# A float32 encoder trunk on one core: x read over two queues, one more block of it evicted by two engines, and the last down projection's right half summed onto the residual in PSUM

## What is computed

```python
def _rmsnorm(x, g):
    xf = x.astype(jnp.float32)
    y = xf * lax.rsqrt(jnp.mean(xf * xf, axis=-1, keepdims=True) + EPS)
    return (y * g.astype(jnp.float32)).astype(x.dtype)

for layer in range(DEPTH):
    h = _rmsnorm(x, mix_norm[layer])
    x = x + mixer(h)                 # attention in layer 0, recurrence in layer 1
    x = x + _swiglu(_rmsnorm(x, ffn_norm[layer]), ffn_w_gate_up[layer], ffn_w_down[layer])
return _rmsnorm(x, final_norm)
```

## Time and profile before

| what | value |
|---|---|
| median of three runs | 1302.98 us (1302.68 to 1303.4) |
| the profiled execution's own time | 1301.03 us |
| its span in the trace | 1299.2 us |
| PE busy | 1282.9 us, 99% |
| PEld (weight load) busy | 1028.2 us, 79% |
| POOL busy | 611.0 us, 47% |
| DVE busy | 560.6 us, 43% |
| ACT busy | 551.7 us, 42% |
| DRAM traffic | 97 GB/s over the span |

### The profile page before, as it was taken

How to read it: one execution, slowest core, us unless ns; L and a number is a source line. 1 busy time by engine, 2 the same in 40 slices (tenths; PEclk the granted TensorE clock), 3 DMA queues, 4 the chain that set the end, 5 groups by cost and what they waited for, 6 DMA issues and landing times.

```text
span 1299.2 us, 18386 instructions
## 1 busy us (share of the span) xinstructions
PE 1282.9 (99%) x6525; PEld 1028.2 (79%) x6525; DVE 560.6 (43%) x872; ACT 551.7 (42%) x1006; POOL 611.0 (47%) x487
## 2 busy tenths in 40 slices
PE   8999999999999999999999999999999999999998
PEld 6877777777778888888888876777888888888886
DVE  4866574756645512121202027999843131311011
ACT  5454444444445433333323247785533333333223
POOL 4565664646535454545444443430244444444442
PEclk9999999999999999999999999999999999999999
DMA  6522222122323333333332343214333333343322
GB/s 208 160 73 62 68 60 63 56 68 62 121 69 110 97 97 95 96 95 96 102 96 84 106 166 117 81 57 146 98 97 89 105 89 103 91 120 98 96 95 94
DMA packets 123415, 126.31 MB, mean 97 GB/s; under 512 B 7896, under 2 KB 106456, under 8 KB 122712
## 3 DMA queue, kind: packets, MB, share of 16 engines
q1 hardware_dynamic: 123320, 125.46, 32.0%
q10 hardware_dynamic: 32, 0.01, 0.0%
HBM read 119.15 MB, written 6.29 MB: 97 GB/s over the span
## 4 chain that ended last, share of the span: by engine, by line
PE 58%; issue 21%; POOL 12%; DVE 5%; ACT 3%; DMA 1%; POOLq 0%; SPq 0%; DVEq 0%; ACTq 0%
PE ps L1493 17%; PE ps L1495 16%; PE ps L1494 16%; POOL w_lo L495 11%; PE ps L1853 2%; PE ps L1611 1%; PE ps L1646 1%; PE ps L1623 1%; PE ps L1627 1%; PE ps L1588 1%; POOL rot L504 1%; PE ps L1657 1%; DMA x_tok<-in_x_dram 1%; PE ps L1665 1%; DVE bkn L1137 1%
## 5 line engine op out<-in xcount | busy, mean ns | idle before, releaser
L495 POOL TENSOR_TENSOR w_lo<-w_stage,w_hi 128x512 fp32r<-128x512 f32 (+2 forms) x430 | 543.0, 1267 | 672.6 <-ACT w_hi L555 672.4
L555 ACT ACTIVATE w_hi<-w_stage 128x512 fp32r<-128x512 f32 (+2 forms) x448 | 263.8, 594 | 574.4 <-PE ps L1495 565.2
L1493 PE MATMUL ps<-h_hi,w_hi 128*128 128x512 f32 x1104 | 439.8, 398 | 1.6 <-DVE h_lo L948 1.0
L1495 PE MATMUL ps<-h_hi,w_lo 128*128 128x512 f32 x1104 | 430.2, 390 | 0.0
L1494 PE MATMUL ps<-h_lo,w_hi 128*128 128x512 f32 x1104 | 430.1, 390 | 0.0
L1493 PEld LDWEIGHTS ps<-h_hi,w_hi 128*128 128x128 f32 x1104 | 207.3, 188 | 63.4 <-issue 16.7
L1495 PEld LDWEIGHTS ps<-h_hi,w_lo 128*128 128x128 f32 x1104 | 207.2, 188 | 43.6
L1494 PEld LDWEIGHTS ps<-h_lo,w_hi 128*128 128x128 f32 x1104 | 207.4, 188 | 43.2 <-issue 2.6
L1276 DVE TENSOR_TENSOR silu_g<-ps,rstd_wide 128x512 f32<-128x512 f32 x44 | 30.2, 686 | 327.5 <-PE ps L1495 327.5
L1493 PE MATMUL ps<-w_hi,f_hi 128*128 128x512 f32 x176 | 68.6, 390 | 0.1
L1495 PE MATMUL ps<-w_hi,f_lo 128*128 128x512 f32 x176 | 68.5, 389 | 0.0
(11 more groups left out here) (229 smaller groups left out, 1633.6 us busy)
## 6 DMA issues: line engine op xcount, KB each, us to landing
w_stage<-in_ffn_w_gate_up_dram SPq DMA_DIRECT2D x176, 256.0 KB, 3.1
w_stage<-in_ffn_w_down_dram SPq DMA_DIRECT2D x88, 256.0 KB, 2.7
w_stage<-in_even_w_in_dram SPq DMA_DIRECT2D x96, 192.0 KB, 2.5
w_stage<-in_odd_w_in_dram SPq DMA_DIRECT2D x32, 256.0 KB, 2.8
x_spill<-x_t SPq DMA_DIRECT2D x2, 2048.0 KB, 8.5
x_t<-x_spill SPq DMA_DIRECT2D x2, 2048.0 KB, 7.9
w_stage<-in_odd_w_out_dram SPq DMA_DIRECT2D x16, 256.0 KB, 2.7
w_stage<-in_even_w_out_dram SPq DMA_DIRECT2D x16, 192.0 KB, 2.4
```

The costliest lines, as they stand in the source:

```text
L495: pool.tensor_tensor(out=w_lo[:, s, 0:n], in0=stage[:, s, 0:n], in1=w_hi[:, s, 0:n].bitcast(f32), op=ALU.subtract).then_inc(chunk_lo, 1)
L555: act.activation(w_hi[:, j % RING, 0:n], stage[:, j % RING, 0:n], ACT.Copy).then_inc(chunk_hi, 1)
L1493: pe.matmul(out_, lh, rh, start=start, stop=False, skip_group_check=skip)
L1495: return pe.matmul(out_, ll, rh, start=False, stop=stop, skip_group_check=skip)
```

## The change

There are four parts.

1. SP issues x blocks 0 and 2, ACT's queue blocks 1 and 3, ahead of `mix_rows`. The turn of `mix_rows` on PE stands behind x_turn(1).
2. Block 2 of x_t is copied in halves like block 3, the left by DVE and the right by ACT.
3. ACT converts chunk 4 behind the first square of x and chunk 5 behind the second.
4. Only the left four tiles of the residual are turned back in the first group of the last FFN, into banks 2 and 3 by turns. The right four tiles are turned during the half g = 0 of the last down projection, at k = 8 to 11, straight into banks 4 to 7 (`x_under_sums`), and the products of g = 1 are accumulated onto them. So `y_sum(1, c)` goes, and the square and the scaling of the right half read PSUM.

```diff
@@ -388,7 +388,7 @@
 
             sync.dma_start(ident[:, :], A["consts"][:, K_IDENT:K_IDENT + P]).then_inc(consts_in, 16)
-            for c in range(NC):
+            for c in (0, 2):
                 sync.dma_start(x_tok[:, c, :], x_rows[c]).then_inc(x_in[c], 16)
             for c in range(C_PAIR):
@@ -420,7 +420,7 @@
                     if (p, j) == (0, 3):
                         sync.wait_ge(x_by_dve, 3)
-                        sync.wait_ge(x_by_act, 2)
+                        sync.wait_ge(x_by_act, 3)
                         sync.dma_start(x_spill, x_t[:, :, :].rearrange("p k t -> p (k t)")).then_inc(spilled, 16)
 
@@ -584,10 +584,13 @@
 
                 g, c = divmod(i, NC)
-                act.wait_ge(y_new, i + 1)
+                if g:
+                    act.wait_ge(y_summed, c + 1)
+                else:
+                    act.wait_ge(y_new, c + 1)
                 if i >= 2:
                     act.wait_ge(y_squared, i - 1)
-                act.activation(y_sq[:, i % 2, :], y_tok[c][:, g * 512:(g + 1) * 512], ACT.Square,
+                act.activation(y_sq[:, i % 2, :], ps[:, 4 + c, :] if g else y_tok[c][:, 0:512], ACT.Square,
                                accum_out=y_stat[:, g, c:c + 1]).then_inc(y_squared, 1)
 
@@ -626,6 +629,8 @@
                 act.activation(rstd_wide[:, :], ps[:, NORM_BANK[n], :], ACT.Sqrt, scale=1.0 / D, bias=eps[:, 0:1]).then_inc(norm_sqrt, 1)
 
+            for c in (1, 3):
+                act.dma_start(x_tok[:, c, :], x_rows[c]).then_inc(x_in[c], 16)
             act.dma_start(mix_rows[0:G_FFN, :], A["mix_norm"].rearrange("l (n p) -> (l n) p", p=P)).then_inc(mix_in, 16)
 
@@ -636,7 +641,7 @@
                     act.wait_ge(mix_gain_in, 1)
                     act.wait_ge(x_by_dve, 3)
-                act.wait_ge(x_by_act, 1 + k // 4)
+                act.wait_ge(x_by_act, 1 + 2 * (k // 4))
                 act.activation(h_hi[:, k, :], x_t[:, k, :], ACT.Copy, scale=params[:, G_MIX + k:G_MIX + k + 1]).then_inc(h_hi_done, 1)
 
@@ -648,6 +653,8 @@
             act.wait_ge(x_turned, 2)
             act.activation(x_t[:, :, P:2 * P], ps[:, 2:4, :].rearrange("p b (j t) -> p (b j) t", t=P), ACT.Copy).then_inc(x_by_act, 1)
+            act.wait_ge(x_turned, 3)
+            act.activation(x_t[:, 4:8, 2 * P:3 * P], ps[:, 5, :].rearrange("p (j t) -> p j t", t=P), ACT.Copy).then_inc(x_by_act, 1)
             convs(0, 1)
             act.wait_ge(x_turned, 4)
@@ -662,8 +669,8 @@
                     act.wait_ge(first_ss, c)
                 act.activation(x_sq[:, :], x_tok[:, c, :], ACT.Square, accum_out=rstd[:, c:c + 1]).then_inc(first_ss, 1)
-                if c == 1:
-                    convs(4, 6)
+                if c < 2:
+                    convs(4 + c, 5 + c)
             act.wait_ge(first_ms, 1)
             act.activation(rstd[:, :], rstd[:, :], ACT.Sqrt).then_inc(first_sqrt, 1)
@@ -936,11 +943,12 @@
                                        src.to_broadcast([P, n, P]), ALU.mult)
 
-            def x_in_place(c):
+            def x_in_place(c, tiles):
 
                 dve.wait_ge(x_turned, c + 1)
                 b0 = 4 if c == 2 else 6
-                V.tensor_copy(x_t[:, :, c * P:(c + 1) * P], ps[:, b0:b0 + 2, :].rearrange("p b (j t) -> p (b j) t", t=P)).then_inc(x_by_dve, 1)
+                src = ps[:, b0:b0 + tiles // 4, :].rearrange("p b (j t) -> p (b j) t", t=P)
+                V.tensor_copy(x_t[:, 0:tiles, c * P:(c + 1) * P], src).then_inc(x_by_dve, 1)
 
             def raw_low(k):
@@ -958,12 +966,11 @@
                 V.tensor_tensor(h_lo[:, k, :], h_f[:, k % 3, :], h_hi[:, k, :].bitcast(f32), ALU.subtract).then_inc(h_lo_done, 1)
 
-            x_in_place(0)
+            x_in_place(0, KD)
             dve.wait_ge(mix_turned, 1)
             V.tensor_copy(params[:, 0:G_FFN], ps[:, 1, 0:G_FFN]).then_inc(mix_gain_in, 1)
-            x_in_place(2)
-            dve.wait_ge(x_turned, 4)
-            V.tensor_copy(x_t[:, 0:4, 3 * P:4 * P], ps[:, 6, :].rearrange("p (j t) -> p j t", t=P)).then_inc(x_by_dve, 1)
+            x_in_place(2, 4)
+            x_in_place(3, 4)
             for k in range(KD):
                 raw_low(k)
@@ -1228,18 +1235,17 @@
 
                 dve.wait_ge(x_tok_turned, c + 1)
-                V.tensor_copy(y_tok[c][:, :].rearrange("p (b t) -> p b t", b=2), ps[:, 2:4, :]).then_inc(x_tok_in, 1)
-
-            def y_sum(g, c):
-
-                t = slice(g * 512, (g + 1) * 512)
-                V.tensor_tensor(y_tok[c][:, t], y_tok[c][:, t], ps[:, 4 * g + c, :], ALU.add).then_inc(y_new, 1)
+                V.tensor_copy(y_tok[c][:, 0:512], ps[:, 2 + c % 2, :]).then_inc(x_tok_in, 1)
+
+            def y_sum(c):
+
+                V.tensor_tensor(y_tok[c][:, 0:512], y_tok[c][:, 0:512], ps[:, c, :], ALU.add).then_inc(y_new, 1)
 
             def finish(c_left):
                 dve.wait_ge(chunk_used, c_left)
                 for c in range(NC):
-                    y_sum(0, c)
+                    y_sum(c)
                 dve.wait_ge(y_squared, NC)
                 dve.wait_ge(gain_in, 16)
@@ -1247,12 +1253,10 @@
                 dve.wait_ge(y_gained, NC)
                 for c in range(NC):
-                    dve.wait_ge(y_summed, c + 1)
-                    y_sum(1, c)
                     dve.wait_ge(y_root, c + 1)
                     V.reciprocal(rstd[:, c:c + 1], rstd[:, c:c + 1]).then_inc(y_scale, 1)
                     dve.wait_ge(y_scale, c + 1)
-                    V.scalar_tensor_tensor(out=y_tok[c][:, 512:D], in0=y_tok[c][:, 512:D], scalar=rstd[:, c:c + 1],
+                    V.scalar_tensor_tensor(out=y_tok[c][:, 512:D], in0=ps[:, 4 + c, :], scalar=rstd[:, c:c + 1],
                                            in1=final_gain[:, 512:D], op0=ALU.mult, op1=ALU.mult).then_inc(y_right, 1)
 
@@ -1517,9 +1521,9 @@
             pe.wait_ge(consts_in, 16)
             x_turn(0)
+            x_turn(1)
             pe.wait_ge(mix_in, 16)
             pe.transpose(ps[:, 1, 0:G_FFN], mix_rows[0:G_FFN, :], ident[0:G_FFN, 0:G_FFN]).then_inc(mix_turned, 1)
-            x_turn(1)
             x_turn(2)
             x_turn(3)
@@ -1754,11 +1758,20 @@
                 if c == 0:
                     pe.wait_ge(x_new, 3 * KD)
-                else:
-                    pe.wait_ge(x_tok_in, c)
-                for j in range(KD):
-                    last = pe.transpose(ps[:, 2 + j // 4, (j % 4) * P:(j % 4 + 1) * P], x_t[:, j, c * P:(c + 1) * P], ident[:, :])
+                if c >= 2:
+                    pe.wait_ge(x_tok_in, c - 1)
+                for j in range(4):
+                    last = pe.transpose(ps[:, 2 + c % 2, j * P:(j + 1) * P], x_t[:, j, c * P:(c + 1) * P], ident[:, :])
                 last.then_inc(x_tok_turned, 1)
+
+
+            def x_under_sums(c):
+
+                if c == 0:
+                    pe.wait_ge(f_ready, 2 * KF)
+                for j in range(4):
+                    pe.matmul(ps[:, 4 + c, j * P:(j + 1) * P], x_t[:, 4 + j, c * P:(c + 1) * P], ident[:, :], start=j == 0, stop=False,
+                              is_transpose=True, skip_group_check=True)
 
             def ffn(n, nn, h_base, fb):
@@ -1812,7 +1825,7 @@
                         s = (cd + k) % RING
                         return mm3(ps[:, 4 * g + c, :], f_hi[:, k, c * P:(c + 1) * P], f_lo[:, k, c * P:(c + 1) * P],
-                                   w_hi[:, s, :], w_lo[:, s, :], k == 0, k == KF - 1)
+                                   w_hi[:, s, :], w_lo[:, s, :], k == 0 and g == 0, k == KF - 1, g == 1)
 
                     if n == 1:
@@ -1823,6 +1836,8 @@
                                 last = tokens(k, c)
                             last.then_inc(chunk_used, 1)
+                            if g == 0 and 8 <= k < 8 + NC:
+                                x_under_sums(k - 8)
                         if g == 1:
                             for c in range(NC):
```

## The result

| | before | changed |
|---|---|---|
| median of 22 runs each | 1302.36 us | 1304.15 us |
| lowest, highest | 1300.62, 1305.33 | 1300.74, 1305.63 |
| profiled execution, its span | 1301.03, 1299.2 | 1303.86, 1302.1 |

The ratio is 1.0014 with a 95% interval of 1.0008 to 1.0019: the changed kernel is slower by about 1.8 us. That is less than the 0.2% that I called the least that can be told, but with 22 runs each it is clear of noise. The forecast was 1302.6 us, within 1301.3 to 1303.9: the measured time lies above the range, and it went the other way.

A forecast was written before the change was run, and what follows sets the result against it. PE's work, the stretch before its first product and the stretch after its last were taken as the bound. Terms -0.75 + 0.36 - 0.53 + 0.5 = -0.42 took the median from 1302.98 to 1302.6 us, range 1301.3 to 1303.9.

The forecast's parts named there:

- Term 1: Behind the last product: DVE's addition leaves the chain and ACT's square starts earlier, reading PSUM; -0.75 us.
- Term 2: Step back to tokens: turning in eight pieces instead of four adds four switches of 0.09 on PE; +0.36 us.
- Term 3: Third step: chunk 4 converted one square earlier removes PE's wait for w_lo, chunk 6 just in time; -0.53 us.
- Term 4: Head: last x load lands 0.46 earlier, but two turns remain behind it and ACT's copies queue; +0.5 us.
- rival B: Head: late mix_rows holds two turns, or block 0 lands late sharing with block 1; +1.3 us, chance 0.25.
- rival C: Head: PE's longer pause before the first turn drops its clock; about 2 us on the path, chance 0.05.

The follow-up runs named there:

- e13: The changed kernel with six more products of zeros in the head and ten unread products at the recurrence gates' pause; median 1300.82 us.
- e14: The kernel before with six more products of zeros in the head and ten unread products at the recurrence gates' pause; median 1301.16 us.
- e1: The changed kernel with 14 instead of 8 products of zeros ahead of PE's first turn; median 1302.33 us.
- e6: The kernel before with only chunk 4's conversion one square earlier; median 1302.19 us.
- e7: The kernel before with ten unread products filling PE's pause at the recurrence gates; median 1301.43 us.
- e8: The changed kernel with all x loads on SP, mix_rows first on ACT's queue, and ten unread products at the gates' pause; median 1300.31 us, ratio 0.9987.
- e15: The changed kernel with x blocks 0 and 2 on ACT's queue, 1 and 3 on SP's, nothing filled; median 1301.25 us, ratio 0.9990.

## Why the prediction was wrong

**The sum of the four terms was about right.** It was -0.42; with the clock held the change is worth -0.34 in the medians and -0.37 in the profiled executions (e13 against e14), and -0.21 against the unfilled profiled execution before. What moved the median by +1.79 is what the sum left out.

**Term 1, the end: right.** -0.75 was forecast, -0.76 measured. From the start of the last product to the end of the span it is 6.3 us in each of the five traces of kernels with the old end, and 5.5 in all twelve with the new one. (The -0.68 in my expectations came from spans rounded to 0.1 us.) The square reads PSUM in 0.60 us (0.59 forecast), starts 0.03 behind the last product's end, and DVE's scaling from PSUM takes 0.75 as from SBUF.

**Term 2, eight pieces: right in kind.** +0.36 forecast, +0.25 measured. The four pieces under the sums cost 1.94 us, just what half of an eight and a switch of 0.09 make four times over. The four taken out of the first group save 1.69 (the lag goes from 3.33 to 1.64) where the same reckoning has 1.58: a group of four holds the next product for 0.35, less than half of the 0.79 of eight.

**Term 3, chunk 4: right.** -0.53 forecast, -0.58 measured, and chunk 6 is just in time, as forecast: in the changed kernel the product that needs it starts 0.28 behind the one ahead and not 0.23.

```profile
27.62 0.39 PE L1499 MATMUL ps<-h_hi,w_lo 128*128 128x512 f32 x1
27.90 0.47 PE L1497 MATMUL ps<-h_hi,w_hi 128*128 128x512 f32 x1
```

**Term 4, how x comes in: the step that failed.** It said +0.5, and it took the clock to stay up through the head. It was +2.16, of which 1.58 is the fall of the clock and 0.58 the late first turn. With the clock held it is +0.68 (e13 against e14) to +0.88 (e1). Two things were wrong in it. First, the path: I followed the last landing and assumed that PE's first turn would be at about 6.9, though I had rival B's remark that block 0 shares the engines with block 1. The last x load was in at 8.9, earlier than the 9.33 that I gave it, and PE did not wait for it. The first turn was at 7.49, and four turns back to back from there make the 0.58; the landings of blocks 2 and 3 and of `mix_rows` held nothing up. That the term came near the measured size with the clock held is luck, since another load sets it. Nor did blocks 0 and 1 land together: they landed 2.5 us apart. Rival B named a late head too (+1.3), but for the wrong reason: `mix_rows` was there in time. The Trainium skill (DMA: Bandwidth & Descriptors, "Issuing engines are not separate DMA queues") says that such loads interleave. The trace agrees in that the landings of the two queues alternate (blocks 1, 0, 3, 2), and what this costs is the time of the load that is needed first.

Second, **rival C was the case, and I gave it 0.05.** It had the place (the pause ahead of the first turn), the sign and about the price (+2; measured 1.58 in the traces, 1.61 in the medians). What I got wrong is its weight. The only fall I had seen stood at the end of the trace, and I read the head before, at 1.00 throughout, as safe. e6 shows that old head without its clock, behind a pause of 1.77 us. The forecast itself had a pause of some 1.8 us, from 5.1 to 6.9, so the fall could strike it even as I drew it; the pause became 2.39. I wrote "2 to 3" into the rival and left it at one in twenty.

**The range.** It took the spread from three runs, 0.7 us. 22 runs spread over 4.7. The profiled execution before happened to have the gates' pause without a fall; a row with 2.7 us of idle PE was there to be seen among PE's waits, and I passed it over, since the change does not touch it.

**What the medians say.** The median moved by +1.79 where the change with the clock held is worth -0.34 to -0.21. So the falls cost the median 2.0 to 2.1 us more than before. A fall in the head is worth 1.6. What makes up the rest was not shown. Filled, the changed kernel takes 1300.8, and two falls make it 1303.9; seven of its 22 runs are at 1303.9 to 1304.3, but nine are at 1304.9 to 1305.6, a further microsecond up. A clock that rises late, as in e7 and e8, is a candidate; no trace of the changed kernel shows one.

## What to carry to other kernels

Before you let two loads run side by side, ask which of them somebody waits for: put that one first on the queue that starts first. A pause of PE of one to three microseconds can cost more than the pause, as those of 1.2 to 2.7 us did here, and whether it does varies from execution to execution, so look for such pauses in the whole trace, fill them with products nobody reads, and only then compare versions that differ by half a microsecond. A trace without a fall is one draw, not a proof.

## What the runs showed of the hardware

- The same program loses its clock in some executions and not in others. Over 149 runs of the kernel before, 50 were at or under 1301.5 us, 92 between 1301.5 and 1303.5 and 7 above; one more, at 2545.3, twice the time of all others, is left out. With both pauses filled, 23 runs of the changed kernel on two chips lay within 0.6 us.
- Six products of zeros (128x512) bought 1.6 us in the head, and ten products bought 1.5 us at the gates (1.7 between the traces), where the eight float32 products of a step take 3.67 us at 2.4 GHz and 5.37 when most of them run at 1.2. The Trainium skill (TensorE: Matmul & The Clock Gate, "The HAM clock gate") has idleness take the clock down and activity bring it back; these runs agree.
- There are three kinds of head. With x on SP, the first product starts at 12.6 to 13.4 when the clock rises and stays, at 14.8 when it rises and falls again (e6), and at 14.6 and 15.8 when it rises late and the turns run at half rate (e8, e7).
- When two loads of 512 KB run side by side, the one behind can land far later. Block 0 on SP behind `ident`, with block 1 issued some 0.5 us earlier on ACT's queue, was turned at 7.49 to 7.78; as the first load of ACT's queue it was turned at 5.61 (e15).
- Transposes that open an accumulation, with split float32 products summed onto them in PSUM, run at the pace of plain ones (0.35 us for four until the next product), and the sum needs no copy and no addition.
